# One-core transformer kernel: three root-mean-square factors applied behind the products, value products moved ahead of the last head mean

## The reference, cut to what matters

```python
def rms_norm(x, gain):                   # also _rmsnorm
    return x * lax.rsqrt(mean(x * x, axis=-1) + 1e-6) * gain

# first block, start: h = rms_norm(x, norm_mix); proj = h @ w_in
#   the q and k heads are normed per head, the v columns are used as they are
# end of the first block, the "sigmoid layer":
h = rms_norm(x, norm_ple)
x = x + sigmoid(h @ w_ple_gate) * (p @ w_ple)
# second block, layer 0:
h = rms_norm(x, norm_mix_2[0])
q, k, v, u = split(h @ ab_w_in)          # differential attention on q, k, v; pooling on u
# second block, layer 1, behind a feed-forward layer:
h = rms_norm(x, norm_mix_2[1])
q, k, v, g_out, gk_low = split(h @ gla_w_in)   # linear attention; silu(g_out) gates its output
```

## Time and profile before

| | us |
|---|---|
| runs, median (lowest to highest) | 3413.21 (3407.13 to 3416.47), 3 runs |
| the profiled execution, its own time | 3407.41 |
| its span, first to last instruction | 3405.6 |
| PE busy | 3298.0 (97%) |
| DVE, POOL, ACT busy | 1767.8, 1347.1, 1323.0 |
| mean granted PE clock | 0.987 of full speed |

### The profile page before, as it was taken

How to read it: one execution, slowest core, us unless ns; L and a number is a source line. 1 busy time by engine, 2 the same in 40 slices (tenths; PEclk the granted TensorE clock), 3 DMA queues, 4 the chain that set the end, 5 groups by cost and what they waited for, 6 DMA issues and landing times.

```text
span 3405.6 us, 41327 instructions
## 1 busy us (share of the span) xinstructions
PE 3298.0 (97%) x15280; PEld 2663.0 (78%) x15280; DVE 1767.8 (52%) x3041; ACT 1323.0 (39%) x2177; POOL 1347.1 (40%) x582
## 2 busy tenths in 40 slices
PE   8999998999999999999999999898999999999998
PEld 5687777888888888888888887576888878788886
DVE  6815226999999951355555563426311135652212
ACT  4434223335777753322222222335322234433221
POOL 4520233344344444444444444245444433434442
PEclk9999999999999999999999999899999999999999
DMA  3230222344556466666666664221233321123232
GB/s 113 74 124 13 87 94 78 109 147 130 186 203 220 170 227 192 186 189 185 187 188 190 187 185 121 71 99 50 93 96 96 93 91 69 38 81 93 93 96 84
DMA packets 424825, 428.08 MB, mean 126 GB/s; under 512 B 146512, under 2 KB 343760, under 8 KB 423008
## 3 DMA queue, kind: packets, MB, share of 16 engines
q1 hardware_dynamic: 424672, 426.00, 39.7%
HBM read 354.63 MB, written 69.21 MB: 124 GB/s over the span
## 4 chain that ended last, share of the span: by engine, by line
PE 76%; issue 13%; POOL 6%; DVE 3%; DMA 2%; ACT 1%; POOLq 0%; SPq 0%; DVEq 0%; PEldq 0%; ACTq 0%
PE pb L660 23%; PE pb L662 22%; PE pb L661 22%; POOL s_over L584 5%; PE pb L941 2%; PE pb L865 1%; DMA s_ring<-eu 1%; PE pb L850 1%; PE pb L828 1%; PE pb L962 1%; DMA s_ring<-w 1%; PE pb L732 0%; PE pb L838 0%; PE pb L892 0%; PE pb L867 0%
## 5 line engine op out<-in xcount | busy, mean ns | idle before, releaser
L584 POOL TENSOR_TENSOR s_over<-s_ring,s_rhigh 128x1024 fp32r<-128x1024 f32 x518 | 1274.2, 2461 | 1991.4 <-ACT s_rhigh L1230 1991.2
L1230 ACT ACTIVATE s_rhigh<-s_ring 128x1024 fp32r<-128x1024 f32 x518 | 548.1, 1059 | 1269.1 <-DMA s_ring<-w 552.0
L660 PE MATMUL pb<-s_over,s_rhigh 128*128 128x512 f32 x2112 | 834.9, 395 | 0.0
L662 PE MATMUL pb<-s_over,s_over 128*128 128x512 f32 x2112 | 833.8, 395 | 0.0
L661 PE MATMUL pb<-s_over,s_rhigh 128*128 128x512 f32 x2112 | 833.7, 395 | 0.0
L660 PE MATMUL pb<-s_hS,s_rhigh 128*128 128x512 f32 (+1 forms) x1888 | 754.0, 399 | 42.0 <-DVE s_hS L1673 23.0
L662 PE MATMUL pb<-s_hS,s_over 128*128 128x512 f32 (+1 forms) x1896 | 736.6, 389 | 0.0
L661 PE MATMUL pb<-s_hS,s_rhigh 128*128 128x512 f32 (+1 forms) x1888 | 733.3, 388 | 0.0
L1819 DVE TENSOR_TENSOR s_xT<-pb,s_xT 128x512 f32<-128x512 f32 x216 | 149.4, 692 | 630.7 <-PE pb L662 630.7
L661 PEld LDWEIGHTS pb<-s_over,s_rhigh 128*128 128x128 f32 x2112 | 397.2, 188 | 95.4 <-issue 0.7
L660 PEld LDWEIGHTS pb<-s_over,s_rhigh 128*128 128x128 f32 x2112 | 397.2, 188 | 95.0 <-issue 0.7
(11 more groups left out here) (268 smaller groups left out, 2853.4 us busy)
## 6 DMA issues: line engine op xcount, KB each, us to landing
s_ring<-w SPq DMA_DIRECT2D x272, 512.0 KB, 3.2
s_ring<-eu SPq DMA_DIRECT2D x128, 512.0 KB, 3.8
s_ring<-ev SPq DMA_DIRECT2D x128, 512.0 KB, 4.1
acts<-s_arena SPq DMA_DIRECT2D x128, 256.0 KB, 3.9
gates<-s_arena SPq DMA_DIRECT2D x8, 4096.0 KB, 13.6
s_arena<-acts SPq DMA_DIRECT2D x128, 256.0 KB, 4.3
s_arena<-gates SPq DMA_DIRECT2D x128, 256.0 KB, 4.5
s_xT<-xT SPq DMA_DIRECT2D x4, 512.0 KB, 7.3
```

The source lines that it names most:

```text
L584: gp.tensor_tensor(rlow[:, s, :, :], ring[:, s, :, :], rhigh[:, s, :, :].bitcast(F32), ALU.subtract).then_inc(S("w_split"), 1)
L660: mm(dst, a_high, b_high, start=start, stop=False)
L662: return mm(dst, a_low, b_high, start=False, stop=stop)
L1230: sc.activation(rhigh[:, s, :, :], ring[:, s, :, :], ACT.Copy).then_inc(S("w_high"), 1)
```

## The change

Five edits; the diff is cut to its core. What it shows for T_AB is done for T_GLA alike (with `hS` and `norm(5)`), and the factor's turn after tile 17 is L752's code, moved.

1. The norms k = 2 (sigmoid layer), 3 (differential attention) and 5 (linear attention) take the form of k = 4 and 6. `plain` on ACT writes gain * x (high part) and squares; `low_plain` on DVE writes the low part. Norms 2 and 5 write `hS`, norm 3 writes `hF`, which the products of T_AB then read. PE does the mean behind the p products (k = 2) or behind the first tile (k = 3, 5). The factor is applied: by DVE to each gate tile, ahead of the sigmoid (`e_scaled`); by DVE to q and k, in place of ACT's copies; by ACT to v, with a column of factors (`r_col`) that PE turns (`turn_root`) and ACT copies (`column`); by POOL to the four pooling tiles and the eight gate tiles of linear attention; by DVE to the low-rank gate.
2. `pT` gets a place of its own in the arena, and its load stands ahead of the last 12 expert tiles. The p products of the first half come ahead of the mean, and those of the second half wait for `xT` one by one.
3. The value products: PE turns the factor after tile 17, and the first two value products stand ahead of the last head mean. They use banks 5 and 4 in place of 6 and 7.
4. The four loads for linear attention's gate (gkw, gku, scan, lev) stand behind 4 tiles of T_GLA in place of 8; the two memsets stand ahead of the factor, and the split of gkw stands in the middle of the q and k results.
5. Semaphores that only DVE uses are merged in `own_step`, two of POOL's in `pool_a`. `r_col` (8 words) lies behind the arena, whose size stays.

```diff
@@ sync
+            sp.dma_start(pT, a["pT"]).then_inc(S("p_in"), 16)
...
             tiles(T_PLE, T_PLE + RING, W_PLE)
-            sp.wait_ge(S("x_upd"), X_PEER)
-            sp.dma_start(pT, a["pT"]).then_inc(S("p_in"), 16)
...
-            tiles(T_GLA, T_GLA + 8, W_GLA)
+            tiles(T_GLA, T_GLA + 4, W_GLA)
             sp.wait_ge(S("x_upd"), X_F0)
...
@@ gpsimd
+                gp.wait_ge(S("rstd_done"), 4)
+                gp.tensor_tensor(src, src, r_row, ALU.mult).then_inc(S("pool_a"), 1)
...
-            splits(T_F0, T_GLO + RING)
+            splits(T_F0, T_GLA + 16 + RING)
+            gp.wait_ge(S("rstd_done"), 6)
+            for n in range(DC):
+                gp.wait_ge(S("lg_copied"), n + 1)
+                gp.tensor_tensor(lg[:, n, :], lg[:, n, :], r_row, ALU.mult).then_inc(S("lg_normed"), 1)
+                splits(T_GLA + 16 + RING + n, T_GLA + 16 + RING + n + 1)
@@ tensor
+            def turn_root(k):
+                pe.wait_ge(S("rstd_done"), k + 1)
+                for t in range(TT):
+                    m = mm(pb[:, 6, t:t + 1], rstd[0:1, 0, t * P:(t + 1) * P], mats[0:1, M_ID, 0:1],
+                           start=t == 0, stop=t == TT - 1)
+                m.then_inc(S("r_turned"), 1)
...
+                if i == 17:
...
+                if i == 20:
+                    pe.wait_ge(S("h_by_u"), 2 * DC)
+                    pe.wait_ge(S("r_copied"), 1)
+                    value(0)
+                    value(1)
...
-            norm(2)
             pe.wait_ge(S("p_in"), 16)
             for half in range(2):
                 w = slot(T_PLE + 5 * half)
-                if half:
-                    pe.wait_ge(S("x_upd"), X_PEER + 4)
                 for o in range(4):
-                    if half == 0 and o == 3:
-                        pe.wait_ge(S("std_done"), 3)
+                    if half:
+                        pe.wait_ge(S("x_upd"), X_PEER + o + 1)
                     for c in range(2):
                         m = mm(pb[:, o, :], ring[:, w, o * 2 + c, :], pT[:, c, :], start=c == 0, stop=c == 1)
                 m.then_inc(S("tile_done"), 1)
+                if half == 0:
+                    norm(2)
                 for o in range(4):
                     if half == 1:
-                        pe.wait_ge(S("e_sig"), o + 1)
+                        pe.wait_ge(S("e_scaled"), o + 1)
+                    elif o == 3:
+                        pe.wait_ge(S("std_done"), 3)
                     linear(T_PLE + 5 * half + 1 + o, 4 + o, hwait=H_NORM[2] if half == 0 and o == 0 else None)
-            norm(3)
-
+            pe.wait_ge(S("x_upd"), X_PEER + 5)
             for i in range(8):
                 if i >= 4:
-                    pe.wait_ge(S("d_copied"), i - 3)
-                linear(T_AB + i, i % 4, hwait=H_NORM[3] if i == 0 else None)
+                    pe.wait_ge(S("qk_out"), i - 3)
+                linear(T_AB + i, i % 4, h=hF, hwait=H_NORM[3] if i == 0 else None)
+                if i == 0:
+                    norm(3)
+                if i == 4:
+                    turn_root(3)
+            pe.wait_ge(S("r_copied"), 2)
...
@@ scalar
+            def plain(k, c, x_before, dst):
+                sc.wait_ge(S("x_upd"), x_before - 7 + c)
+                sc.activation(dst[:, 0, c, :], xT[:, c, :], ACT.Identity, scale=col(C_GAIN + 8 * k + c))\
+                    .then_inc(S("h_high"), 1)
+                square(k, c, x_before)
+            def column(k):
+                sc.wait_ge(S("r_turned"), k + 1)
+                sc.activation(r_col[:, 0:TT], pb[:, 6, 0:TT], ACT.Copy).then_inc(S("r_copied"), 1)
+                sc.wait_ge(S("r_copied"), k + 1)
...
             mean_root(2)
-            highs(2)
             for o in range(DC):
                 parts(T_PLE + 4 + o + (o >= 4))
-                sc.wait_ge(S("tile_done"), T_PLE + 2 + o + (o >= 4))
-                sc.activation(esig[:, o % 2, :], pb[:, 4 + o % 4, :], ACT.Sigmoid).then_inc(S("e_sig"), 1)
-                if o >= 1:
-                    square(3, o - 1, X_PLE)
+                sc.wait_ge(S("e_scaled"), o + 1)
+                sc.activation(esig[:, o % 2, :], esig[:, o % 2, :], ACT.Sigmoid).then_inc(S("e_sig"), 1)
+                if o >= 1:
+                    plain(3, o - 1, X_PLE, hF)
...
-            highs(3)
-            for i in range(8):
-                parts(T_AB + i + 3)
+            parts(T_AB + 10)
+            column(1)
...
@@ vector
+            low_plain(2, 7, hS)
+            invert_root(2)
             for o in range(DC):
+                ve.wait_ge(S("tile_done"), T_PLE + 2 + o + (o >= 4))
+                ve.tensor_tensor(esig[:, o % 2, :], pb[:, 4 + o % 4, :], r_row, ALU.mult).then_inc(S("e_scaled"), 1)
                 ve.wait_ge(S("e_sig"), o + 1)
                 ve.tensor_tensor(et[:, o % 2, :], pb[:, o % 4, :], esig[:, o % 2, :], ALU.mult)
                 ve.tensor_tensor(xT[:, o, :], xT[:, o, :], et[:, o % 2, :], ALU.add).then_inc(S("x_upd"), 1)
+                if o >= 1:
+                    low_plain(3, o - 1, hF)
+                if o >= 2:
+                    sum_square(3, o - 1)
-            norm(3)
+            low_plain(3, 7, hF)
+            invert_root(3)
...
+            for i in range(8):
+                dst3 = dq[:, i, :] if i < 4 else dk[:, i - 4, :]
+                ve.wait_ge(S("tile_done"), T_AB + i + 1)
+                ve.scalar_tensor_tensor(dst3, pb[:, i % 4, :], 0.125 if i < 4 else 1.0, r_row, ALU.mult, ALU.mult)
...
```

More of the change, by code:

```diff
@@ L109, in raw @@
 def raw(n):
-    return n - DC * sum(h < n for h in (H_NORM[0], H_CAT, H_NORM[4]))
+    return n - DC * sum(h < n for h in (H_NORM[0], H_NORM[2], H_NORM[3], H_CAT, H_NORM[4], H_NORM[5], H_NORM[6]))
 X_MIX = 8
@@ L570, in _ @@
             sp.dma_start(lev, a["c_lev"]).then_inc(S("lev_in"), 16)
-            tiles(T_GLA + 8, T_GLA + 32, W_GLA + 8)
+            tiles(T_GLA + 4, T_GLA + 32, W_GLA + 4)
             ffn(1, T_F1)
@@ L720, in _, with value @@
                 mean_square(c)
-            for i in range(22):
+            def value(n):
+                k, t = divmod(n, TT)
+                tile0 = (T_VD12, T_VD12 + 2, T_VA, T_VA + 2, T_VD0)[k]
+                if n >= 2:
+                    pe.wait_ge(S("v_copied"), n - 1)
+                h = hu if k < 2 else (hS[:, 0, :, :], hS[:, 1, :, :])
+                by_token(pb[:, 5 - n % 2, 0:2 * P], tile0, tokens_of(t), h).then_inc(S("v_done"), 1)
+                if t == TT - 1:
+                    pe.wait_ge(S("v_done"), n + 1)
+                    pe.sem_inc(S("tile_done"), 2)
+            for i in range(21):
                 if 1 <= i < 20:
@@ L727, in _ @@
                     linear(T_QKD + i, QK_BANK[i % 4])
+                if i == 17:
+                    pe.wait_ge(S("rope_sin"), 12)
+                    for b in range(2 * TT):
+                        tok = slice(b * P, (b + 1) * P) if b < TT else slice(b - TT, T, 4)
+                        m = mm(pb[:, 4, b:b + 1], rstd[0:1, 0, tok], mats[0:1, M_ID, 0:1], start=True, stop=True)
+                    m.then_inc(S("r_turned"), 1)
+                if i == 20:
[3 more added lines that the diff above has]
+                    value(1)
                 if 1 <= i <= 20:
@@ L1085, in _ @@
                 linear(T_GLA + i, i % 4, hwait=H_NORM[5] if i == 0 else None)
+                if i == 0:
+                    norm(5)
+                if i == 4:
+                    turn_root(5)
+            pe.wait_ge(S("r_copied"), 3)
             pe.wait_ge(S("gkw_split"), 2)
@@ L1296, in _ @@
                 r = r_tok[:, t + TT:t + TT + 1] if n < 2 * TT else r_tok[:, t:t + 1]
-                sc.activation(dst, pb[:, 6 + n % 2, 0:2 * P], ACT.Identity, scale=r).then_inc(S("v_copied"), 1)
+                sc.activation(dst, pb[:, 5 - n % 2, 0:2 * P], ACT.Identity, scale=r).then_inc(S("v_copied"), 1)
             def attention(n, s0, exp, pt, beside=None):
@@ L1434, in norm_plain @@
                     parts(t0 - 5 + c)
-                    sc.wait_ge(S("x_upd"), x0 - 7 + c)
-                    sc.activation(hF[:, 0, c, :], xT[:, c, :], ACT.Identity, scale=col(C_GAIN + 8 * k + c))\
-                        .then_inc(S("h_high"), 1)
-                    square(k, c, x0)
+                    plain(k, c, x0, hF)
                 mean_root(k)
@@ L1485, in _ @@
                 h = n // TT * 2 * P
-                sc.activation(dv[:, n % TT, h:h + 2 * P], pb[:, 4 + n % 4, 0:2 * P], ACT.Copy)\
+                sc.activation(dv[:, n % TT, h:h + 2 * P], pb[:, 4 + n % 4, 0:2 * P], ACT.Identity,
+                              scale=r_col[:, n % TT:n % TT + 1])\
                     .then_inc(S("d_copied"), 1)
@@ L1553, in _ @@
             mean_root(5)
-            highs(5)
-            for i in range(8):
-                parts(T_GLA + i + 3)
-                sc.wait_ge(S("tile_done"), T_GLA + i + 1)
-                dst2 = lq[:, i, :] if i < 4 else lk[:, i - 4, :]
```

(9 more changed lines are left out.)

166 lines of the change are left out of this document (84 added, 82 removed).

## The result

| | before | after |
|---|---|---|
| median of 4 runs, us | 3411.4 (3407.1 to 3416.5) | 3375.6 (3369.8 to 3380.5) |
| the profiled execution, us | 3407.4 | 3370.9 |
| its span, us | 3405.6 | 3369.1 |
| ratio of the times | | 0.9894, 95% interval 0.9868 to 0.9919 |

3372 was forecast, from 3413.2; the difference is 35.8 us between the medians and 36.5 between the two spans, where the sum said 40.5.

What follows compares the result with a forecast made beforehand. PE, busy 97% of the span, was taken as the bound. Terms -9.2 - 22.6 - 10.4 + 1.4 + 0.3 = -40.5 us, from the median 3413.2, gave 3372.7, say 3372; 8-in-10 range 3360 to 3387.

Steps and rivals of the forecast that it cites:

- Where time could come from: Whole kernel: PE busy 97%, so only its own work or its stops; a stop also costs slow matmuls behind it.
- Part 1: Value products, mean 19 to value 2: 21.6 us before, 11.8 rebuilt at full rate, gain 9.2 us (7.5 to 10.5).
- the pause behind mean 20: PE waits there for value copy 0: 2.4 us, plus 0.6 for a possible clock drop.
- Part 2: Sigmoid layer with the q and k tiles (T_AB): 130.5 us before, 107.9 after, gain 22.6 us (20 to 25).
- the expected stop of 0.6 in front of T_AB's chunk 7: T_AB's first tile reaches chunk 7 4.8 us after gate tile 7; DVE needs 5.4, so PE stops 0.6.
- Part 3: Linear attention's first tiles (T_GLA): 57.1 us before, 46.7 after without a stop, gain 10.4 us (9 to 11).
- The pooling multiply: POOL's added multiply on the pooling tiles: exposed only for the last one, 1.3 plus hand-off, +1.4 us.
- this mechanism as a rival: Sigmoid layer's gate tiles: POOL splits block DVE operations with two SBUF inputs, DVE becomes the bound; +10.4 us, 3382, chance 0.12.
- Its sign of it: Sign for the added pooling multiply: PE's wait for POOL ahead of the fourth pooling product is 2.4 us.
- Linear attention's end: Behind linear attention's first tiles, up to the kernel's end: no change forecast, 0 us.
- v copies: ACT's v copies with a column of factors cost 0.47 each; only the last of each series shows, +0.3 us together.
- From sum to median: Whole kernel: the sum is taken from the median shown, 3413.2; a median of few runs moves by a few us more.

Runs made afterwards that it cites:

- stop_back: The kernel after, but PE waits for norm 5's inverted root ahead of the first linear-attention tile; ratio to the kernel before 0.9933 (0.9917 to 0.9949).
- value_back: The kernel after with value products and factor's turn put back behind the last mean; span 3377.8 us, ratio to the kernel before 0.9908.
- Part 1 alone: The kernel before with only the factor's turn at tile 17 and value products 0 and 1 ahead of the last mean; 3402.0 us against 3408.2, ratio 0.9982.

## Why the prediction was right, step by step

- *Where time could come from.* Right. Every one of the named stops was real, and its removal paid, because PE had work for the freed time. Measuring a stage from start to start, instead of adding waits, is what made the sizes fit: the wait for norm 5 was 6.5 us, its stage gave 10.6, and stop_back shows that a stop of 6.9 and 1.2 us alone costs 10.2.
- *Part 1, 9.2 us (7.5 to 10.5).* Too large. Value 2 started at 173.5 instead of 171.9 (181.1 less 9.2), and was copied at 178.2 instead of 174.4: the turn took 2.8 us and not 1.9, and the clock fell behind it (1.7 us up to the next mean), which the sum had only for the pause behind mean 20. That pause was 2.0 (forecast 2.4), but the slow products behind it cost 1.5 us, not 0.6 (value 2 takes 4.5 us; the 5.9 that an expectation calls slow holds the pause itself). Of 7.5 us at value 2, 4.3 were left at value 18, behind three new waits of 0.4 to 0.6 us for copies; 2.8 more came up to norm 1's mean, where the granted clock was 0.82 to 0.84 from 260 to 300 us before and 1.00 after, and 1.6 up to the experts' end. The 2.8 can't be put down to part 1: from value 18 to norm 1's mean value_back, with the old order, takes 288.2 us, and the three kernels with the new order and the same long stop take 288.1 to 288.2. So that 8.7 lies near 9.2 is luck. Part 1 alone measures 6.1 us.
- *Part 2, 22.6 us.* 23.7. DVE's chain per tile is 4.1 us (4.4 forecast), and the expected stop of 0.6 in front of T_AB's chunk 7 did not come. From start to start the p products took 13.3 us (14.7 in the sum) and the two norms' means 2.6 (3.7), while the 16 tiles took 89.9 (88.0): terms that were off by up to 1.9 us and partly cancel. No wait for POOL's splits or for words. No run undoes part 2 alone: that the gain is the stops is read from the timelines. In this stretch of before PE stood still for 2.6, 3.4, 3.3 and 6.5 us and 2.0 in shorter waits, 17.7 in all; in after it did not, and the clock is at its upper level throughout.
- *Part 3, 10.4 us.* 10.6.
- *The pooling multiply, +1.4.* The term that failed: 3.4. I had POOL's chain right (from the last pooling tile to the last product 1.45 us more) and left out that POOL's operations block DVE's. The prediction had this mechanism as a rival, but looked for it at the splits beside the gate tiles, where it cost nothing, and not at the operation that was added itself, beside the softmax that PE waits for. Its sign of it, PE's wait for POOL at 2.4 us, was wrong too: the wait fell to 0.65, because PE itself came later.
- *Linear attention's end, 0.* 2.3 us lost between the two profiled executions, but by the averages of C over all profiles 0.3: the 0 was as good as can be told. What ACT's chain of absolute value, exponential and logarithm sets is the start of value 4, 24 us behind the low-rank product in both kernels; PE's wait there (1.8 and 3.35) is short or long with either form of the norms.
- *v copies, +0.3.* Nothing in the differential attention.
- *From sum to median.* Within 4 us, partly by luck: by the table above the gain fell short by 5.6 us in four stretches (pooling 2.0, linear attention's end 2.3, feed-forward 0.8, part 1 0.5) and was 1.6 larger in three. The range of 3360 to 3387 holds all of after's runs.

## What to carry to other kernels

A stop of the engine that bounds the kernel costs more than its idle time: measure the stretch from start to start, and expect the gain of its removal to shrink again at the next wait whose end is fixed by another chain. Before a few us between two profiles are given a cause, look how far the same instructions differ among all profiles. Price an added operation on POOL not only by its own chain but by each DVE operation on SBUF that it will meet, the small ones too. On an in-order engine put what waits for a transfer behind what another engine waits for, but no later than its own reader allows.

## What the runs showed that I had not expected

- One wait with two lengths: the first of two words landed 3.4 or 6.3 us behind its issue, with 16 small transfers sent behind it each time, and ACT's order turned that into a stop of PE of 1.1 or 4.4 us.
- A DVE operation on 128x2 took 1.78 us instead of 0.17 beside a POOL split: what counts is not the length of the DVE operation but what is left of POOL's.
- 16 one-column products took 2.8 us, 0.18 each, not the 0.117 of the 128x128 ones, and the granted clock averaged 0.76 in the 7 us from their start, though PE was busy all the time.
